# An earlier place for the first attention scores, the query and key norms and the first output unit in a two-block float32 kernel

## The chip, the cores and the metric

One core of a Trainium2 chip runs the whole program in one launch. The metric is the device time of one execution in microseconds; the median over several executions is compared. The five engines named below are TensorE (matrix products into PSUM), VectorE, ScalarE, GpSimd and SyncE (which here only issues DMAs). Each has a queue of its own, worked in the order written; they meet at semaphores.

## The reference

The reference is float32 throughout, on 256 tokens of width 1024. A first block has two layers, a second block one; each is a mixer followed by a gated feed-forward layer (SwiGLU, hidden width 2816), with RMS norms and residuals. The change lies in the first layer's mixer, `hybrid_mixer`:

```python
proj = h @ w_in
gq, gk, gv, gr, glr, sq, sk, sv = jnp.split(proj, cuts, axis=-1)
o_gla = gla_mixer(gq, gk, gv, gr, glr, w_gate2, b_gate, g_gla)
o_sb = stick_breaking_mixer(sq, sk, sv, g_q, g_k)
o = jnp.concatenate([o_gla, o_sb], axis=-1)
return o @ w_out
```

`gla_mixer` is a gated linear attention with 4 heads, chunks of 64, an RMS norm over each head's output and a gate `silu(r)`. `stick_breaking_mixer` has 8 heads of 64 and is computed like this, for blocks of 128 queries:

```python
qh = _rms_f32(heads(q), g_q) * (SB_HEAD_DIM ** -0.5)
kh = _rms_f32(heads(k), g_k)
z = jnp.einsum('bhtd,bhsd->bhts', qh[:, :, q0:kv_len], kh[:, :, :kv_len])
log_keep = jnp.where(past, jax.nn.log_sigmoid(-z), 0.0)
between = lax.cumsum(log_keep, axis=3, reverse=True) - log_keep
w = jnp.where(past, jnp.exp(jax.nn.log_sigmoid(z) + between), 0.0)
outs.append(jnp.einsum('bhts,bhsd->bhtd', w, vh[:, :, :kv_len]))
```

## The kernel before, in words

**Weights.** All weights come as a stream of units of 128 x 2048 float32 (1 MB). SyncE loads unit u into one of two raw slots once VectorE has made the low half of unit u - 2 (`lo_done`, L1089). ScalarE then copies it to a rounded high half (`hi`, L260), which for units from 3 on waits until TensorE has finished unit u - 2 (`unit_done`, L259), since there are three slots. VectorE subtracts to give the low half (`lo`, L264). Each product is done three times, high by high, high by low and low by high (L277 to L279), to keep float32 precision. A unit of projections or output has two halves of 24 products each.

**The stages around the change.** Units 0 to 11 are the projections (`in1`), 12 to 15 the output matrix of the mixer (`out1(0)` to `out1(3)`), and from 16 on the feed-forward layer. The stick-breaking heads are worked in four pairs g. Projections 8 and 9 hold the keys of the pairs and 10 and 11 the queries, two pairs to a unit. These four units are numbered j = 0 to 3 in `qk_ss`, `qk_rstd` and `qk_norm` ("the sums j = 3", "factor 3"; the norm of unit 11 is j = 3). The scores of pairs 0 and 1 need j = 0 and 2, those of pairs 2 and 3 need j = 1 and 3.

- `qk_ss(j)` (L1154): TensorE sums the squares of 64 rows, one product of 512 columns. `qk_rstd(j)` (L1701): ScalarE takes Ln and Exp (L1704, L1707), "factor j". `qk_norm(j)` (L2108): VectorE scales projection 8 + j into `QKN` (L2112). Before that VectorE copies the projection out of PSUM (`copy_proj`, L2105), and the squares are made by ScalarE (`qk_square`, L1698) or, for j = 3, by VectorE (L2167).
- The GLA output `OG` is squared by ScalarE (L1747), summed by TensorE (L1215, "the GLA sums"), goes through Ln and Exp (L1752, L1754) on ScalarE, and is scaled and gated on VectorE (L2162, L2174); `gla_high(j)` (L2206) makes the high half of a quarter of the mixer's output.
- `sb_z(g)` (L1221): scores of pair g into PSUM banks `SB_BANK[g]` and the next. `sb_log(g)` (L1759): Abs, Exp and Ln on ScalarE (L1765, L1768, L1770), "logs g". `sb_keep(g)` (L2181): VectorE, two operations (L2187, L2190), "keep". `sb_between(g)` (L1239): TensorE adds the sums over later keys (L1242, L1244), "the correction" (the first is g = 0, the third g = 2). `sb_logs(g)` (L2192): VectorE (L2196), "log g". `sb_weights(g)` (L1772): Exp on ScalarE (L1774). `sb_out(g)` (L1248): weights times values on TensorE; `sb_store(g)` (L1778): ScalarE copies it into `MIX`.
- `mix_split_lo(dve, 0, (q,))` (L660): the low half of MIX quarter q. `out1(j, ks)` (L1260): the products of output unit j for the input tiles ks, two tiles to a quarter, 12 products to a quarter; it waits for that quarter's low half and for the unit's low half (L1263).
- `idle_products(7, 10)` (L1278): ten bfloat16 products on zeros into a bank that nobody reads.

**What sets the order.** Nothing is scheduled by a program: each engine's order is written out by hand, TensorE's at L1210 to L1299, ScalarE's at L1740 to L1800, VectorE's at L2157 to L2225. After it, the residual of each output unit is added by VectorE (L2247), which with ScalarE also makes the operands of the feed-forward layer (L452, L569). GpSimd issues its first loads (L2602 to L2605) when the last quarter of the mixer's output is there (`act_lo` at 8, L2600).

Of the kernel before, what the change touches and what calls it, by code (L numbers as in the profile page):

```python
# [74 lines left out]
def program(nc, A):  # L75
# [6 lines left out]
    with ExitStack() as ctx:  # L82
        sems = {}

        def S(name):
            if name not in sems:
                sems[name] = ctx.enter_context(nc.semaphore(name))
            return sems[name]
# [47 lines left out]
        def banks(a, b):  # L136
            return PS[:, a:b, :].rearrange("p b n -> p (b n)")
# [129 lines left out]
        def hi(act, u):  # L267
            if u < UNITS:
                split_hi(act, u, u % SLOTS, u % RAW_SLOTS, u // RAW_SLOTS + 1)
# [11 lines left out]
        def idle_products(bank, n):  # L281

            for _ in range(n):
                nc.tensor.matmul(PS[:, bank, :], zero[:, 0:P], zero, start=True, stop=True)
# [60 lines left out]
        FOLDED = {0: "mixn0", 1: "ffnn0", 2: "mixn1", 3: "ffnn1"}  # L345
        HALF = {0: 0, 1: 0, 2: 0, 3: 0}
        MIX_HALF = (1, 0)
        OUT1_BANK = (7, 2, 3, 0)
        SB_BANK = (0, 2, 4, 0)
        NORM_HN = {4: 0, 5: 1, 6: 2}  # L350
        NORM_ROW = {4: 0}
        BACK_BANK = ((5, 7, 0, 2), (4, 5, 7, 6))
# [746 lines left out]
        def _(pe):  # L1099
# [42 lines left out]
            def in1(u, middle=None):  # L1142

                pe.wait_ge(S("lo_done"), u + 1)
                if u >= 4:
                    pe.wait_ge(S(f"proj{u % 2}_copied"), u // 2)
                outs = [PS[:, IN1_BANK(u), t * T:(t + 1) * T] for t in range(2)]
                if u in (6, 7):
                    last = token_unit(u % SLOTS, [(0, t, outs[t]) for t in range(2)], None, middle)
                else:  # L1150
                    last = feature_unit(u % SLOTS, outs, 0, middle=middle)
                last.then_inc(S("unit_done"), 1)

            def qk_ss(j):  # L1154

                pe.wait_ge(S("qk_sq"), j + 1)
                if j == 0:
                    pe.wait_ge(S("norm_rs"), 1)
                if j == 1:
                    pe.wait_ge(S("qk_rs"), 1)  # L1160
                if j >= 2:
                    pe.wait_ge(S(f"proj{j % 2}_copied"), 6)
                nc.tensor.matmul(PS[:, QK_BANK[j], :], blk, SQF[:, j * 512:(j + 1) * 512], start=True, stop=True)\
                    .then_inc(S("qk_ss"), 1)
# [43 lines left out]
                                         start=True, stop=True)  # L1208
            i.then_inc(S("gla_mm"), 1)
            qk_ss(0)  # L1210
            in1(10)

            pe.wait_ge(S("gla_act"), 5)
            for e in range(2):
                i = nc.tensor.matmul(PS[:, e, :], ones, OR[:, e * 512:(e + 1) * 512], start=True, stop=True)  # L1215
            i.then_inc(S("gla_mm"), 1)
            qk_ss(1)
            in1(11, middle=lambda: qk_ss(2))


            def sb_z(g):  # L1221
                if g == 0:
                    pe.wait_ge(S("qkn_done"), 3)
                    pe.wait_ge(S("og_rs"), 1)
                if g == 1:
                    pe.wait_ge(S("gla_act"), 4)
                if g == 2:
                    pe.wait_ge(S("qkn_done"), 4)
                if g == 3:
                    pe.wait_ge(S("sb_lz2"), 1)  # L1230
                for e in range(2):
                    r, b = half(e), SB_BANK[g] + e
                    kT, qT = QKN[r, g * T:(g + 1) * T], QKN[r, 1024 + g * T:1024 + (g + 1) * T]
                    nc.tensor.matmul(PS[:, b, 0:256], kT[:, 0:P], qT, start=True, stop=False, skip_group_check=True)
                    i = nc.tensor.matmul(PS[:, b, 256:384], kT[:, P:T], qT[:, P:T], start=False, stop=False,
                                         skip_group_check=True)
                i.then_inc(S("sb_z"), 1)

            def sb_between(g):  # L1239
                pe.wait_ge(S("sb_keep"), g + 1)  # L1240
                for e in range(2):
                    nc.tensor.matmul(PS[:, SB_BANK[g] + e, 0:384], minus, SBM[:, g % 2, e, :], start=False, stop=False,  # L1242
                                     skip_group_check=True)
                    i = nc.tensor.matmul(PS[:, SB_BANK[g] + e, 128:256], minus_all, SBM[:, g % 2, e, 256:384],  # L1244
                                         start=False, stop=True, skip_group_check=True)
                i.then_inc(S("sb_between"), 1)
# [13 lines left out]
            def out1(j, ks, blocks=range(2)):  # L1260

                u, b = U_OUT1 + j, OUT1_BANK[j]
                pe.wait_ge(S("lo_done"), u + 1)  # L1263
                if 0 in ks and j:
                    pe.wait_ge(S("sb_lz2"), 4 if j == 3 else 2)
                for nb in blocks:
                    for k in ks:
                        wait_act(pe, "o1", k)
                        H, L = wblk(u % SLOTS, nb * KT + k)
                        i = split_mm(PS[:, b, nb * T:(nb + 1) * T], H, L, a_hi[:, k, 1, :], a_lo[:, k, 1, :],  # L1270
                                     k + nb == 0, k == KT - 1, skip_group_check=True)
                if KT - 1 in ks:
                    i.then_inc(S("unit_done"), 1)

            sb_z(0)
            sb_z(1)
            qk_ss(3)
            idle_products(7, 10)  # L1278
            sb_between(0)
            sb_z(2)  # L1280
            sb_z(3)
            sb_out(0)
# [8 lines left out]
            out1(0, (4, 5))  # L1291
            out1(1, (4, 5))
            sb_out(3)
            out1(2, range(4))
            out1(2, (4, 5))
            for j in range(3):
                out1(j, (6, 7))
            out1(3, range(KT))
            ffn_pe(pe, 0, "ffn0", 1)  # L1299

# [345 lines left out]
        def _(act):  # L1646
# [49 lines left out]
            def qk_square(j):  # L1696
                act.wait_ge(S(f"proj{j % 2}_copied"), (8 + j) // 2 + 1)
                nc.scalar.activation(SQF[:, j * 512:(j + 1) * 512], PROJ[:, 8 + j, :], ACT.Square)\  # L1698
                    .then_inc(S("qk_sq"), 1)

            def qk_rstd(j):  # L1701
                r = RSF[:, j * 512:(j + 1) * 512]
                act.wait_ge(S("qk_ss"), j + 1)
                nc.scalar.activation(r, PS[:, QK_BANK[j], :], ACT.Ln, scale=1.0 / 64, bias=prm_eps)\  # L1704
                    .then_inc(S("qk_rs"), 1)
                act.wait_ge(S("qk_rs"), 2 * j + 1)
                nc.scalar.activation(r, r, ACT.Exp, scale=-0.5).then_inc(S("qk_rs"), 1)  # L1707
# [38 lines left out]
            act.wait_ge(S("gla_act"), 4)  # L1746
            nc.scalar.activation(OR, OG, ACT.Square).then_inc(S("gla_act"), 1)  # L1747
            qk_rstd(0)
            qk_square(2)
            hi(act, 13)  # L1750
            act.wait_ge(S("gla_mm"), GLA_MM["sums"])
            nc.scalar.activation(OR, banks(0, 2), ACT.Ln, scale=1.0 / P, bias=prm_eps).then_inc(S("og_rs"), 1)  # L1752
            act.wait_ge(S("og_rs"), 1)
            nc.scalar.activation(OR, OR, ACT.Exp, scale=-0.5).then_inc(S("og_rs"), 1)  # L1754
            qk_rstd(1)
            qk_rstd(2)


            def sb_log(g):  # L1759

                l = SBL[:, g % 2]
                act.wait_ge(S("sb_z"), g + 1)
                if g >= 2:
                    act.wait_ge(S("sb_v"), g - 1)
                nc.scalar.activation(l, PS[:, SB_BANK[g]:SB_BANK[g] + 2, 0:384], ACT.Abs)\  # L1765
                    .then_inc(S("sb_a"), 1)
                act.wait_ge(S("sb_a"), 3 * g + 1)
                nc.scalar.activation(l, l, ACT.Exp, scale=-1.0).then_inc(S("sb_a"), 1)  # L1768
                act.wait_ge(S("sb_a"), 3 * g + 2)
                nc.scalar.activation(l, l, ACT.Ln, bias=1.0).then_inc(S("sb_a"), 1)  # L1770
# [11 lines left out]
                act.wait_ge(S("sb_o_read"), 2 * (j - 1))  # L1782

            sb_log(0)
            qk_rstd(3)
            sb_log(1)
            sb_weights(0)
            sb_log(2)
            sb_weights(1)
            sb_store(0)  # L1790
# [274 lines left out]
        def _(dve):  # L2065
# [91 lines left out]
            lo(dve, 12)  # L2157
            copy_proj(10)
            qk_norm(0)
            lo(dve, 13)  # L2160
            dve.wait_ge(S("og_rs"), 2)
            dve.scalar_tensor_tensor(OG, OG, prm("glan"), OR, ALU.mult, ALU.mult).then_inc(S("gla_step"), 1)  # L2162
            qk_norm(1)
            qk_norm(2)
            copy_proj(11)
            dve.wait_ge(S("proj1_copied"), 6)
            dve.tensor_tensor(SQF[:, 3 * 512:4 * 512], PROJ[:, 11, :], PROJ[:, 11, :], ALU.mult).then_inc(S("qk_sq"), 1)  # L2167
            dve.wait_ge(S("gla_step"), 3)
            dve.wait_ge(S("gla_act"), 2)
            og = OG.rearrange("p (e a t) -> p a e t", e=2, a=2)  # L2170
# [32 lines left out]
            def gla_high(j):  # L2203
                ks = slice(2 * j, 2 * j + 2)
                dve.wait_ge(S("gla_out"), 1)
                dve.tensor_copy(mix_operands(0, ks)[0], MIX[:, ks, :]).then_inc(S("mix_hi"), 1)  # L2206

            sb_keep(0)
            qk_norm(3)
            gla_high(0)  # L2210
            dve.wait_ge(S("sb_bias"), 2)
            sb_logs(0)
            sb_keep(1)
            gla_high(1)
            mix_split_lo(dve, 0, (0,))
            sb_logs(1)
            mix_split_lo(dve, 0, (1,))
            sb_keep(2)
            sb_logs(2)
            sb_keep(3)  # L2220
# [546 lines left out]
```

## Time and profile before

| | us |
|---|---|
| median of 3 runs | 1015.05 |
| lowest, highest | 1014.77, 1016.3 |
| the profiled execution | 1014.54 |
| its span, first to last instruction | 1012.4 |
| TensorE busy | 995.6 (98%) |
| VectorE busy | 664.4 (66%) |
| ScalarE busy | 489.6 (48%) |
| chain that ended last | TensorE 93%, VectorE 3%, ScalarE 2%, DMA 1% |

Times in the trace count from the start of the span. The rows name an engine (PE is TensorE, PEld its weight loads, DVE VectorE, ACT ScalarE, POOL GpSimd, SPq the DMA queue of SyncE), the line of the kernel, what is written and read, and what ended a wait. Matrix products overlap: a product of 256 columns has a duration of 0.28 us, and the next one starts 0.12 us after it. The granted clock of TensorE is given as a share of full speed, 2.4 GHz.

### The profile page before, as it was taken

Reading aid. Unit: us, or ns where it says so; the run is one execution under the profiler, and the core shown is the slowest. Engines: PE = TensorE matmul, PEld = TensorE weight load, DVE = VectorE, ACT = ScalarE, POOL = GpSimd, SP = SyncE. Lnnn points to the kernel's source line nnn. Section 1 sums busy time; section 2 is a strip of 40 time slices with the busy share of each in tenths; the row PEclk is TensorE's granted clock in tenths of the full one; section 3 lists DMA queues with packets and bytes.
Section 4 is the critical chain, followed back from the end, with each engine's and each line's share of the span. In section 5 each row is a group of like instructions: output and inputs, shape, how many; then the busy total and the mean of one; then the engine's idle time right before and its main releaser. Section 6 shows DMA issues by size and latency. Waiting matters only on the chain.

```text
span 1012.4 us, 14616 instructions
## 1 busy us (share of the span) xinstructions
PE 995.6 (98%) x6164; PEld 845.7 (84%) x6168; DVE 664.4 (66%) x751; ACT 489.6 (48%) x578; POOL 29.7 (3%) x59
## 2 busy tenths in 40 slices
PE   9999999999999999999999999999999999999997
PEld 7997888888888987988888887989978988888886
DVE  5566487767677766767777776434765666666664
ACT  6467474443436533845443547333456454344443
POOL 0000000000000000001010110000000000000000
PEclk9999999999999999999999999999999999999999
DMA  7642367767665654347888883722101435655451
GB/s 268 225 160 91 110 225 271 244 218 254 222 241 187 208 182 129 125 173 272 282 288 276 308 292 119 280 99 91 43 1 43 146 119 184 216 188 206 167 208 42
DMA packets 33751, 187.33 MB, mean 185 GB/s; under 512 B 3744, under 2 KB 7584, under 8 KB 15136
## 3 DMA queue, kind: packets, MB, share of 16 engines
q1 hardware_dynamic: 25344, 154.82, 44.1%
q0 software_dynamic: 7344, 27.79, 7.8%
q10 hardware_dynamic: 1008, 3.94, 1.0%
q8 instruction: 41, 0.67, 0.3%
q14 instruction: 14, 0.11, 0.0%
HBM read 181.41 MB, written 1.05 MB: 180 GB/s over the span
## 4 chain that ended last, share of the span: by engine, by line
PE 93%; DVE 3%; ACT 2%; DMA 1%; issue 0%; SPq 0%; DVEq 0%; ACTq 0%
PE PS L711 11%; PE PS L713 11%; PE PS L712 11%; PE PS L277 7%; PE PS L278 7%; PE PS L279 7%; PE PS L766 6%; PE PS L764 6%; PE PS L765 6%; PE PS L1309 2%; PE PS L744 1%; PE PS L329 1%; PE PS L315 1%; PE PS L330 1%; PE PS L331 1%; DMA raw<-wstream 1%
## 5 line engine op out<-in xcount | busy, mean ns | idle before, releaser
L264 DVE TENSOR_TENSOR w_lo<-raw,w_hi 128x2048 fp32r<-128x2048 f32 x140 | 320.6, 2291 | 174.3 <-ACT w_hi L260 151.7
L260 ACT ACTIVATE w_hi<-raw 128x2048 fp32r<-128x2048 f32 x129 | 246.4, 1912 | 144.0 <-DMA raw<-wstream 110.7
L711 PE MATMUL PS<-w_hi,a_hi 128*128 128x512 f32 x512 | 202.5, 396 | 0.0
L713 PE MATMUL PS<-w_hi,a_lo 128*128 128x512 f32 x512 | 199.8, 390 | 0.0
L712 PE MATMUL PS<-w_lo,a_hi 128*128 128x512 f32 x512 | 199.5, 390 | 0.0
L277 PE MATMUL PS<-a_hi,w_hi 128*128 128x256 f32 (+1 forms) x496 | 150.0, 302 | 1.8 <-DVE w_lo L264 1.5
L278 PE MATMUL PS<-a_lo,w_hi 128*128 128x256 f32 (+1 forms) x496 | 147.1, 297 | 0.0
L279 PE MATMUL PS<-a_hi,w_lo 128*128 128x256 f32 (+1 forms) x496 | 147.0, 296 | 0.0
L713 PEld LDWEIGHTS PS<-w_hi,a_lo 128*128 128x128 f32 x512 | 96.1, 188 | 20.5
L712 PEld LDWEIGHTS PS<-w_lo,a_hi 128*128 128x128 f32 x512 | 96.2, 188 | 19.1
L711 PEld LDWEIGHTS PS<-w_hi,a_hi 128*128 128x128 f32 x512 | 96.2, 188 | 18.8
L764 PE MATMUL PS<-w_hi,h_hi 128*128 128x512 f32 x264 | 103.2, 391 | 0.0
L766 PE MATMUL PS<-w_lo,h_hi 128*128 128x512 f32 x264 | 102.8, 389 | 0.0
L765 PE MATMUL PS<-w_hi,h_lo 128*128 128x512 f32 x264 | 102.7, 389 | 0.0
L277 PEld LDWEIGHTS PS<-a_hi,w_hi 128*128 128x128 f32 x496 | 94.7, 191 | 8.0 <-issue 3.5
L278 PEld LDWEIGHTS PS<-a_lo,w_hi 128*128 128x128 f32 x496 | 94.8, 191 | 3.2 <-issue 0.7
L279 PEld LDWEIGHTS PS<-a_hi,w_lo 128*128 128x128 f32 x496 | 94.8, 191 | 2.5
L937 DVE CUSTOM_DVE_ANT_0 MODJ<-modraw,CROW 128x1024 f32<-128x1024 f32 x64 | 77.9, 1217 | 0.6 <-DMA modraw<-wmod 0.3
L766 PEld LDWEIGHTS PS<-w_lo,h_hi 128*128 128x128 f32 x264 | 49.5, 188 | 10.4
L764 PEld LDWEIGHTS PS<-w_hi,h_hi 128*128 128x128 f32 x264 | 49.6, 188 | 10.3 <-issue 0.2
L765 PEld LDWEIGHTS PS<-w_hi,h_lo 128*128 128x128 f32 x264 | 49.6, 188 | 10.1
L866 ACT ACTIVATE h_hi<-PS 128x512 fp32r<-128x512 f32 x33 | 19.7, 596 | 67.5 <-PE PS L744 67.5
(363 smaller groups left out, 1231.4 us busy)
## 6 DMA issues: line engine op xcount, KB each, us to landing
raw<-wstream SPq DMA_DIRECT2D x141, 1024.0 KB, 4.8
modraw<-wmod POOLq DMA_DIRECT2D x48, 512.0 KB, 5.1
U<-CU SPq DMA_DIRECT2D x28, 142.0 KB, 2.8
cst<-cst ACTq DMA_DIRECT2D x1, 1440.0 KB, 10.2
mlw<-mlw ACTq DMA_DIRECT2D x1, 1280.0 KB, 5.9
X<-xT SPq DMA_DIRECT2D x2, 512.0 KB, 4.9
raw<-wstream SPq DMA_DIRECT2D x2, 512.0 KB, 7.7
CROW<-crow POOLq DMA_DIRECT2D x1, 1024.0 KB, 5.2
```

Source lines behind the costliest of these rows:

```text
L260: nc.scalar.activation(w_hi[:, slot, :], raw[:, rslot, :], ACT.Copy).then_inc(S("hi_done"), 1)
L264: dve.tensor_tensor(w_lo[:, slot, :], raw[:, rslot, :], w_hi[:, slot, :].bitcast(F32), ALU.subtract).then_inc(S("lo_done"), 1)
L277: nc.tensor.matmul(out, H, xh, start=start, stop=False, **kw)
L278: nc.tensor.matmul(out, H, xl, start=False, stop=False, **kw)
L279: return nc.tensor.matmul(out, L, xh, start=False, stop=stop, **kw)
L711: nc.tensor.matmul(out, a_hi[:, k, src, ts], wh, start=k == 0, stop=False, skip_group_check=True)
L712: nc.tensor.matmul(out, a_hi[:, k, src, ts], wl, start=False, stop=False, skip_group_check=True)
L713: i = nc.tensor.matmul(out, a_lo[:, k, src, ts], wh, start=False, stop=k == KT - 1, skip_group_check=True)
L764: nc.tensor.matmul(out, hh, wh, start=False, stop=False, skip_group_check=True)
L765: nc.tensor.matmul(out, hl, wh, start=False, stop=False, skip_group_check=True)
L766: return nc.tensor.matmul(out, hh, wl, start=False, stop=False, skip_group_check=True)
L937: dve.tensor_tensor_reduce(out=MODJ, in0=modraw[:, n % 2, :], in1=CROW[:, c, :], scale=1.0, scalar=0.0, op0=ALU.mult, op1=ALU.add, accum_o ...
```

## The change

On TensorE, the sums j = 1 move from behind unit 10 into its middle, the sums j = 2 from the middle of unit 11 to before it, the scores of pairs 0 and 1 from behind unit 11 into its middle, and the first correction goes ahead of the sums j = 3. The products on zeros are taken out. The last quarter of output unit 0 is done in the middle of output unit 2. The waits of `sb_z` are handed over to match the swapped PSUM banks. On ScalarE, factors 1 and 2 go ahead of the second half of the GLA norm, and the high half of unit 13 and factor 3 go behind logs 1. On VectorE, norms 1 and 2 go ahead of the GLA norm, `gla_high(0)` ahead of the first keep, the copy and squares of unit 11 behind that keep, norm 3 behind the second keep, and the low half of unit 13 behind the low half of MIX quarter 1.

```diff
-        OUT1_BANK = (7, 2, 3, 0)
-        SB_BANK = (0, 2, 4, 0)
+        OUT1_BANK = (7, 0, 1, 2)
+        SB_BANK = (2, 0, 4, 2)
...
             qk_ss(0)
-            in1(10)
+            in1(10, middle=lambda: qk_ss(1))
 
             pe.wait_ge(S("gla_act"), 5)
             for e in range(2):
                 i = nc.tensor.matmul(PS[:, e, :], ones, OR[:, e * 512:(e + 1) * 512], start=True, stop=True)
             i.then_inc(S("gla_mm"), 1)
-            qk_ss(1)
-            in1(11, middle=lambda: qk_ss(2))
-
+            qk_ss(2)
 
             def sb_z(g):
                 if g == 0:
                     pe.wait_ge(S("qkn_done"), 3)
+                    pe.wait_ge(S("gla_act"), 4)
+                if g == 1:
                     pe.wait_ge(S("og_rs"), 1)
-                if g == 1:
-                    pe.wait_ge(S("gla_act"), 4)
                 if g == 2:
                     pe.wait_ge(S("qkn_done"), 4)
...
-            sb_z(0)
-            sb_z(1)
+            def first_two():
+                sb_z(0)
+                sb_z(1)
+
+            in1(11, middle=first_two)
+            sb_between(0)
             qk_ss(3)
-            idle_products(7, 10)
-            sb_between(0)
             sb_z(2)
             sb_z(3)
             sb_out(0)
...
             sb_out(3)
-            out1(2, range(4))
-            out1(2, (4, 5))
-            for j in range(3):
-                out1(j, (6, 7))
+            out1(2, range(3))
+            out1(0, (6, 7))
+            out1(2, range(3, 6))
+            out1(1, (6, 7))
+            out1(2, (6, 7))
             out1(3, range(KT))
             ffn_pe(pe, 0, "ffn0", 1)
...
             nc.scalar.activation(OR, OG, ACT.Square).then_inc(S("gla_act"), 1)
             qk_rstd(0)
+            qk_rstd(1)
             qk_square(2)
-            hi(act, 13)
             act.wait_ge(S("gla_mm"), GLA_MM["sums"])
             nc.scalar.activation(OR, banks(0, 2), ACT.Ln, scale=1.0 / P, bias=prm_eps).then_inc(S("og_rs"), 1)
+            qk_rstd(2)
             act.wait_ge(S("og_rs"), 1)
             nc.scalar.activation(OR, OR, ACT.Exp, scale=-0.5).then_inc(S("og_rs"), 1)
-            qk_rstd(1)
-            qk_rstd(2)
...
             sb_log(0)
+            sb_log(1)
+            hi(act, 13)
+            sb_weights(0)
             qk_rstd(3)
-            sb_log(1)
-            sb_weights(0)
             sb_log(2)
...
             qk_norm(0)
-            lo(dve, 13)
+            qk_norm(1)
+            qk_norm(2)
             dve.wait_ge(S("og_rs"), 2)
             dve.scalar_tensor_tensor(OG, OG, prm("glan"), OR, ALU.mult, ALU.mult).then_inc(S("gla_step"), 1)
-            qk_norm(1)
-            qk_norm(2)
-            copy_proj(11)
-            dve.wait_ge(S("proj1_copied"), 6)
-            dve.tensor_tensor(SQF[:, 3 * 512:4 * 512], PROJ[:, 11, :], PROJ[:, 11, :], ALU.mult).then_inc(S("qk_sq"), 1)
...
+            gla_high(0)
             sb_keep(0)
-            qk_norm(3)
-            gla_high(0)
+            copy_proj(11)
+            dve.wait_ge(S("proj1_copied"), 6)
+            dve.tensor_tensor(SQF[:, 3 * 512:4 * 512], PROJ[:, 11, :], PROJ[:, 11, :], ALU.mult).then_inc(S("qk_sq"), 1)
             dve.wait_ge(S("sb_bias"), 2)
             sb_logs(0)
             sb_keep(1)
+            qk_norm(3)
             gla_high(1)
             mix_split_lo(dve, 0, (0,))
             sb_logs(1)
             mix_split_lo(dve, 0, (1,))
+            lo(dve, 13)
             sb_keep(2)
```

## Rows read from the trace of the kernel before

**Rows 1.** List of waits, TensorE: in total, times, longest (us).
```profile
PE PS L310 <- ACT a_hi L531: 1.6, 1, 1.6
```

**Rows 2.** Timeline of TensorE: start, duration (us), [idle before, releaser].
```profile
93.36 2.10 PE L284 MATMUL PS<-zero 128*128 128x512 bf16 x9
95.89 0.91 PE L1242 MATMUL PS<-SBM,csb 128*128 128x384 f32 x2 [0.43 <-DVE SBM L2190]
...
99.02 0.71 PE L1234 MATMUL PS<-QKN 64*128 64x256 f32 x4 [0.27 <-DVE SBZ L2196]
...
104.44 0.36 PE L277 MATMUL PS<-a_hi,w_hi 128*128 128x256 f32 x1 [0.32 <-DVE a_lo L660]
...
105.95 0.91 PE L1242 MATMUL PS<-SBM,csb 128*128 128x384 f32 x2
...
128.56 0.39 PE L277 MATMUL PS<-a_hi,w_hi 128*128 128x256 f32 x1 [1.52 <-DVE w_lo L264]
...
134.41 0.40 PE L711 MATMUL PS<-w_hi,a_hi 128*128 128x512 f32 x1
```

**Rows 3.** The chain that ended last, in order of time: start, us.
```profile
81.47 1.72 PE PS L1215 x4
83.19 0.86 PE PS L1163 x2
...
97.67 0.23 PE PS L1244 x2
...
102.48 0.23 PE PS L1244 x2
```

**Rows 4.** Timeline of ScalarE, columns as in rows 2.
```profile
84.57 1.10 ACT L1752 ACTIVATE OR<-PS,epsc 128x1024 f32<-128x1024 f32 x1
...
86.67 0.67 ACT L1704 ACTIVATE RSF<-PS,epsc 128x512 f32<-128x512 f32 x1
87.37 0.64 ACT L1707 ACTIVATE RSF<-RSF 128x512 f32<-128x512 f32 x1
...
91.56 0.81 ACT L1765 ACTIVATE SBL<-PS 128x768 f32<-128x768 f32 x1 [2.31 <-PE PS L1235]
...
99.00 0.84 ACT L1774 ACTIVATE SBZ<-SBZ 128x768 f32<-128x768 f32 x1 [1.19 <-DVE SBZ L2196]
...
133.49 1.92 ACT L260 ACTIVATE w_hi<-raw 128x2048 fp32r<-128x2048 f32 x1 [2.87 <-DMA raw<-wstream]
```

**Rows 5.** Timeline of VectorE, columns as in rows 2.
```profile
84.70 2.29 DVE L264 TENSOR_TENSOR w_lo<-raw,w_hi 128x2048 fp32r<-128x2048 f32 x1 [1.84 <-ACT w_hi L260]
...
92.01 1.28 DVE L2174 TENSOR_TENSOR MIX<-OG,RSG 128x512 f32<-128x512 f32 x2
...
94.15 0.96 DVE L2187 SCALAR_TENSOR_TENSOR SBM<-PS,SBL 128x768 f32<-128x768 f32 x1 [0.57 <-ACT SBL L1770]
95.14 0.69 DVE L2190 TENSOR_TENSOR SBM<-SBM,csb 128x512 f32<-128x512 f32 x1
95.75 0.74 DVE L2112 SCALAR_TENSOR_TENSOR QKN<-PROJ,epsc,RSF 128x512 f32<-128x512 f32 x1
...
98.00 0.96 DVE L2196 SCALAR_TENSOR_TENSOR SBZ<-PS,SBBIAS 128x768 f32<-128x768 f32 x1 [1.17 <-PE PS L1244]
...
103.62 0.68 DVE L660 TENSOR_TENSOR a_lo<-MIX,a_hi 128x512 fp32r<-128x512 f32 x1
```

**Rows 6.** DMA issues: size, median us from issue to landing.
```profile
CTX<-ctxT POOLq DMA_DIRECT2D x1, 1024.0 KB, 8.6
```

**Rows 7.** Timeline of TensorE at the start and the end of the span.
```profile
1.21 4.45 PE L284 MATMUL PS<-zero 128*128 128x512 bf16 x10 [1.21 <-DVE epsc L2067]
...
1006.61 0.39 PE L766 MATMUL PS<-w_lo,h_hi 128*128 128x512 f32 x1
```

**Rows 8.** Windows at the end: engines' busy time, granted clock, DMA share, GB/s.
```profile
1010.00:1010.25 0.25, 0.00 (x0) 0.00 (x0) 0.00 (x0) 0.00 (x0) 0.00 (x0) 1.00 1.01 385
...
1010.50:1011.00 0.50, 0.00 (x0) 0.00 (x0) 0.00 (x0) 0.00 (x0) 0.00 (x0) 0.50 1.02 385
```

## The prediction

> **What bounds the kernel now.** The page says that TensorE is busy for 98% of the span, so time can only be won where it waits or runs work that nobody needs. The list of waits comes next: its longest entry for TensorE is 1.6 us [rows 1]. Then TensorE's timeline through the stretch of the change [rows 2], where the waits get their places. It shows 2.10 us of products on zeros from 93.36 (nine of the ten have a record), and the first correction product at 95.89 after a wait of 0.43; then waits of 0.27 at 99.02, 0.32 at 104.44, and 1.52 at 128.56, the last for the low half of weight unit 15. Zero products and waits together are 4.6 us: more than that the change can't win. Last, the chain of waits [rows 3] and the timelines of ScalarE [rows 4] and VectorE [rows 5], for the duration of each step that feeds TensorE. The profiled execution took 1014.54 us around a span of 1012.4; the median of the runs is 1015.05, 0.5 above it. I work out a difference in span and add it to the median.
>
> **What goes.** The zero products go, with the 0.43 behind them: 2.53 us. The 1.52 at 128.56 goes too. Unit 15's high half waits until output unit 0 is finished, then 1.92 us (ScalarE [rows 4]) and 2.29 (VectorE [rows 5]) pass, 4.3 with the hand-overs, before output unit 3 can start. The 48 products of output unit 3 take 128.56 to 134.41, 0.12 each. Before, 24 of them lay over these 4.3 us (2.9); now 42 do, 5.1: covered, with 0.8 us to spare. The new order of the output products costs nothing else.
>
> **Part one: norms forward.** The sums of squares j = 1 move into the middle of unit 10; TensorE's work is the same, unit 10 ends 0.86 later (one such product, 83.19 [rows 3]), at 82.33, and the GLA sums (1.72) at 84.05. The sums j = 2 now follow at once. Their input needs VectorE's copy of unit 10 and ScalarE's square, two operations on 512 columns, like those of 0.6 to 0.75 us in rows 4 and 5: some 1.4 of the 1.72, so it is ready. They end at 84.91, the first half of unit 11 (24 products) at 87.78. Meanwhile ScalarE takes the Ln of the GLA sums (1.10), Ln and Exp of factor 2 (86.67 to 88.00 before, 1.33 [rows 4]) and VectorE the norm (0.74 [rows 5]): from 84.07, ready at 87.2. The first scores don't wait; they end at 88.7 and the second pair's by 89.5, so unit 11 ends at 92.3.
>
> **Part two: the first correction.** From Abs on ScalarE (91.56) to the start of VectorE's keep (94.15) took 2.59 us [rows 4, 5], now 88.68 to 91.27; keep took 94.15 to 95.83, now to 92.95. The GLA gating and its copy, ahead of it on VectorE from 87.4, are two steps like that of 1.28 and short ones, and fit. TensorE, free at 92.3, waits 0.7 and runs the correction from 93.0 to 95.0 (95.89 to 97.90 before [rows 2, 3]). Here the kernel is 2.9 us ahead.
>
> **Part three: what is late next.** TensorE's next two items are the sums j = 3 (0.86, to 95.85) and the scores of pair 2, which need the norm of unit 11. Before, that norm was through at 96.5 [rows 5], while TensorE was in the first correction. Now it stands behind the correction on both engines. ScalarE's queue reads: logs 1 (to 93.7), high half of unit 13 (to 95.5), weights 0, factor 3. Weights 0 wait for VectorE's log 0 (0.96, 95.0 to 95.95) and take 0.84, to 96.8; factor 3 takes 1.33, to 98.1; the norm 0.74, to 98.85. So TensorE stands from 95.85 to 98.9: **3.05 us**. Pair 2's scores start 1.0 later than before (97.90, behind the correction). The whole lead is gone. The 0.27 at 99.02 goes as well: log 0 is done long before.
>
> **Part four: the low half of unit 13.** From pair 3's scores to the end of the second correction took 99.02 to 102.71, 3.69 us [rows 2, 3]; with 0.85 for pair 2's scores (97.90 to 98.75, where the 0.27 at 99.02 begins [rows 2, 3]) ahead of it, that is 98.9 to 103.4. VectorE then has log 1 (0.96), the low part of MIX quarter 1 (0.68), the moved low half of unit 13 (**2.29**, which lay at 84.70, where VectorE would have waited), and only then pair 2's keep (1.68): hand-overs and overlaps included, to 108.7. TensorE has 24 output products in between and the small wait for quarter 1, 3.24 us before (102.71 to 105.95), and is free at 106.65. It waits **2.1 us**, until 108.75; before, the row at 105.95 has no wait. All output products stand behind that one.
>
> **The DMAs and queues.** Unit 15's load waits on SyncE's queue for the low half of unit 13, so it is issued at 107.1 instead of 87.0; a load takes some 5 us (issued at 128.5 and awaited until 133.49 for unit 17 [rows 4]) and this one is wanted at 124.9: hidden, with 13 us to spare. GpSimd's first four loads go with the last output quarter, some 2.8 us later, and are wanted only in the FFN. ScalarE's moved high half of unit 13 lies in time in which ScalarE would wait for log 0: nothing.
>
> **The sum.** The third correction moves from 105.95 to 108.75, +2.8; behind it lies work without a wait up to output unit 3, whose wait of 1.52 goes: +1.3. Counted by waits: new 0.70 + 3.05 + 2.1 = 5.85, gone 2.53 + 0.27 + 1.52 = 4.32, +1.5. The two differ by rounded hand-overs; I take the first, which has fewer terms. Output unit 3 then ends at 135.7 in place of 134.41, and all that follows moves with it: **+1.3 us, 1016.4 us**. The forecast's own range is +0.5 to +2.1 (hand-overs of 0.1 in eight steps), 1015.5 to 1017.2.
>
> **The clock.** The wait of 3.05 is twice the longest of before, and the products that kept TensorE at work are gone. No pause of that length lies within the work. After the last product, which ended at 1007.0, the granted clock stayed at 1.00 until 1010.25 and then fell to 0.50, 1.2 GHz [rows 7, 8]: a pause of 3.25, just longer than this one. What the low clock takes: the ten zero products at the start ran at 0.445 us each, against 0.233 at 93.36 [rows 7, 2], and lasted 4.4 us, so 2.2 of them were lost. Lower bound nothing, upper bound one such stretch for each long wait, 4.4. I take nothing, since 3.05 us lies on the side of rows 7 and 8 that kept the clock. The Trainium skill (TensorE: Matmul & The Clock Gate, "Why this matters for your kernels") speaks against this change: pauses between bursts of products must stay short, or the array goes back to its cold clock. By that rule the change would end near +3.5 instead of +1.3.
>
> **Rivals.** (a) The clock falls in the wait of 3.05. For: nothing fills it any more, and a wait of 0.7 lies shortly before. Against: the row of the end. Time: 1.3 + 2.2, 1018.6; chance 0.22. (b) The FFN's start slips. Unit 17's load is issued at 129.1, when unit 15's low half is done, now in the midst of GpSimd's loads, one of which took 8.6 us to land [rows 6]. At 8.6 it lands at 137.7; high half, low half, the last residual and its operands take 1.9 + 2.3 + 0.7 + 1.8: 144.4. TensorE wants them 30 products of 512 columns after 135.7, at 142.6: 1.8 more, 1018.2. Against: the 5 us landing of before, amid the same traffic. Chance 0.10. (c) Faster: the queues don't bind. If factor 3 and the low half of unit 13 find gaps that I don't see, the new waits fall to 0.7 and the time to 1015.05 + 0.7 - 4.6, 1011.2. It counts as faster once the new waits sum to less than 2.6 us (4.6 less 2.0). Against: both long waits follow from the written order and from rows. Chance 0.07. (d) The new order of products does not relieve unit 15, because a hand-over eats the 0.8 us of cover: up to 1.5 is not won, 1016.4 to 1017.9; chance 0.06. The forecast keeps 0.55.
>
> **Numbers.** A measurement of this kernel tells about 0.2%, 2.0 us, from no change. Faster: (c), 0.07. Slower: (a), (b) and 0.04 from the tail of the forecast and of (d), 0.36. Same: 0.57. The range 1015.0 to 1019.0 takes in the forecast, (a), (b) and (d), and leaves out (c).
>
> **What would show it.** Right: no zero products near 93; waits of TensorE near 3 us ahead of pair 2's scores, for VectorE's norm, and near 2.1 ahead of the third correction, for the keep; none ahead of output unit 3; the FFN's first product near 135.7. Wrong in part four: pair 2's keep done before 106.6. A granted clock under 1.00 between 96 and 110 is (a); a wait in the FFN's second unit is (b). Long waits that sum to under 4.3 us would make the forecast's sign wrong.

## The result and the profile after

| | before | changed |
|---|---|---|
| median of 6 runs, us | 1014.92 | 1020.56 |
| lowest | 1014.64 | 1017.86 |
| ratio, 95% interval | | 1.0046 (1.0036 to 1.0057) |
| profiled execution, its span | 1014.54, 1012.4 | 1020.29, 1018.1 |

The change makes the kernel slower by 0.46%, 4.7 us by the ratio (of mean times), 5.7 us between the two spans. That is outside my range, which ended at 1019.0. Two slow executions, one of the changed kernel (1421.36, mean granted clock 0.653) and a later one of the kernel with both cures (1666.48, 0.556), are in the medians and in no ratio; without the first the changed kernel's median is 1020.29. Between the two profiled executions nearly all of the difference arises in the first 160 us; the table shows how far the changed kernel is behind at five places of TensorE.

| TensorE reaches | before | changed | behind |
|---|---|---|---|
| first sums of squares (j = 0) | 74.6 | 74.4 | -0.2 |
| third correction | 105.95 | 110.30 | 4.35 |
| first product of the FFN | 134.4 | 137.0 | 2.6 |
| first transposes of the FFN | 153.1 | 158.8 | 5.7 |
| last product | 1006.6 | 1012.4 | 5.8 |

First the list of waits of the changed kernel, for TensorE (in total, times, longest, in us):

```profile
PE PS L1232 <- DVE QKN L2113: 3.2, 1, 3.2
PE PS L1240 <- DVE SBM L2187: 2.6, 2, 2.0
PE PS L711 <- DVE a_lo L569: 2.2, 1, 2.2
PE PS L310 <- ACT a_hi L531: 1.6, 1, 1.6
```

Three entries stand above the one that led the list before [rows 1]: the scores of pair 2, the third correction, and the FFN's second unit. TensorE's timeline puts them in place (start, duration, wait before); it answers to [rows 2]:

```profile
92.84 0.91 PE L1240 MATMUL PS<-SBM,csb 128*128 128x384 f32 x2 [0.59 <-DVE SBM L2187]
...
98.85 0.71 PE L1232 MATMUL PS<-QKN 64*128 64x256 f32 x4 [3.15 <-DVE QKN L2113]
...
106.59 0.36 PE L277 MATMUL PS<-a_hi,w_hi 128*128 128x256 f32 x1 [0.32 <-DVE a_lo L660]
...
110.30 0.91 PE L1240 MATMUL PS<-SBM,csb 128*128 128x384 f32 x2 [2.05 <-DVE SBM L2187]
...
137.00 0.40 PE L711 MATMUL PS<-w_hi,a_hi 128*128 128x512 f32 x1
...
144.87 0.47 PE L711 MATMUL PS<-w_hi,a_hi 128*128 128x512 f32 x1 [2.25 <-DVE a_lo L569]
```

The zero products and the wait ahead of output unit 3 are gone. The scores of pair 2 start at 98.85, the very time worked out, after 3.15 us. The third correction waits 2.05, but starts 1.5 later than worked out. What lies between is in the windows (width, busy time of TensorE, its weight loads, VectorE, ScalarE, GpSimd, then the granted clock, DMA share and GB/s):

```profile
96.00:98.00 2.00, 0.00 (x0) 0.00 (x0) 1.46 (x2) 1.97 (x3) 0.00 (x0) 1.00 0.00 0
98.00:100.00 2.00, 1.15 (x11) 1.12 (x13) 1.69 (x3) 0.18 (x2) 0.00 (x0) 0.95 0.03 8
100.00:102.00 2.00, 2.00 (x14) 1.40 (x12) 0.00 (x0) 1.94 (x3) 0.00 (x0) 0.50 0.00 0
102.00:104.00 2.00, 2.00 (x11) 1.30 (x8) 0.00 (x0) 0.40 (x1) 0.00 (x0) 0.70 0.00 0
```

The granted clock fell to 0.50, 1.2 GHz, close to 99.9, **when TensorE had been at work again for a microsecond**, and came back within the last window. ScalarE's timeline shows the third wait's origin, as the row at 133.49 did before [rows 4]:

```profile
139.10 1.92 ACT L260 ACTIVATE w_hi<-raw 128x2048 fp32r<-128x2048 f32 x1 [5.81 <-DMA raw<-wstream]
```

Unit 17 was awaited until 139.10. Its load had been issued behind the low half of unit 15, at 130.7: 8.4 us to landing, in place of 5. The low half of unit 15 on VectorE and the first of GpSimd's loads, before and then changed:

```profile
126.21 2.29 DVE L264 TENSOR_TENSOR w_lo<-raw,w_hi 128x2048 fp32r<-128x2048 f32 x1 [1.25 <-ACT w_hi L260]
120.42 0.66 POOL L2602 DMA_DIRECT2D CROW<-crow  x1 [119.96 <-DVE a_lo L660]
...
128.41 2.29 DVE L264 TENSOR_TENSOR w_lo<-raw,w_hi 128x2048 fp32r<-128x2048 f32 x1 [1.25 <-ACT w_hi L260]
124.78 0.67 POOL L2603 DMA_DIRECT2D CROW<-crow  x1 [124.32 <-DVE a_lo L660]
```

From GpSimd's first load to the issue of unit 17's it was 8.1 us before (120.4 to 128.5) and 5.9 in the changed kernel (124.8 to 130.7).

### The profile page after: what moved, and what is told of

The parts are those of the page before. It is cut to its first block, busy times and chain, and to the rows that moved or that the text cites. A ratio compares the mean times of both kernels' runs of the same rounds, so it can differ in the third digit from the quotient of the medians.

```text
span 1018.1 us, 14597 instructions
## 1 busy us (share of the span) xinstructions
PE 994.3 (98%) x6155; PEld 845.3 (83%) x6158; DVE 664.2 (65%) x751; ACT 490.3 (48%) x578; POOL 29.7 (3%) x59
## 4 chain that ended last, share of the span: by engine, by line
PE 87%; DVE 5%; ACT 4%; DMA 3%; issue 1%; SPq 0%; DVEq 0%; ACTq 0%
PE PS L711 11%; PE PS L713 11%; PE PS L712 11%; PE PS L277 6%; PE PS L279 6%; PE PS L278 6%; PE PS L764 6%; PE PS L766 6%; PE PS L765 6%; DMA raw<-wstream 3%; PE PS L1310 2%; DVE w_lo L264 2%; ACT w_hi L260 1%; PE PS L744 1%; PE PS L315 1%; PE PS L310 1%
```

## The experiments

They form three groups of four, each on one chip, beside the kernel before, whose median was 1016.38, 1015.09 and 1015.24 in the three groups. So I read ratios and profiles, and times only within a group. Theory A from here on: three separate losses, the waits of the written order (+1.3), the clock, and the landing of unit 17.

### Fill the long wait

```diff
             qk_ss(3)
+            idle_products(7, 12)
             sb_z(2)
```

> The changed kernel with twelve products on zeros (2.7 us) in the wait ahead of pair 2's scores. Theory A (the loss has three parts: new waits of the written order +1.3, the clock that falls in the 3.15 us wait +1.5, the late landing of unit 17 +2.3 and more): the granted clock stays at 1.00 up to the end of the third correction, output unit 3 ends 1.3 to 1.6 us earlier than in the changed kernel, the wait in the FFN's second unit stays near 2.2, and the time is 1018.0 to 1019.0. Rival B (all of the loss beyond +1.3 comes of the clock, the FFN's wait with it): the FFN's wait goes too and the time is near 1016.3. Rival C (the fall costs nothing, since other waits take it up): no change, 1020.5.

Ratio 1.0045 (1.0028 to 1.0062), 1020.07 against 1016.38. That misses A's 1018.0 to 1019.0 and by the time alone looks like rival C; but on this chip the kernel before took 1.5 more than in the first measurement. Its timeline of TensorE:

```profile
100.82 0.71 PE L1232 MATMUL PS<-QKN 64*128 64x256 f32 x4 [0.57 <-DVE QKN L2114]
...
110.68 0.91 PE L1240 MATMUL PS<-SBM,csb 128*128 128x384 f32 x2 [2.04 <-DVE SBM L2188]
...
144.95 0.47 PE L711 MATMUL PS<-w_hi,a_hi 128*128 128x512 f32 x1 [1.95 <-DVE a_lo L569]
```

The clock stayed at 1.00. From pair 2's scores to the third correction it took 9.86 us here and 11.45 in the changed kernel (98.85 to 110.30), so this fall cost 1.6 us, which speaks against rival C. The FFN's wait stays at 1.95, which refutes rival B. The intervals of the two kernels overlap, so the gain of filling is shown by the profile and not by the times: this execution had reached its first sums of squares 2.0 us late (76.4), which is nothing of the edit.

### Hold GpSimd's loads back

```diff
             pool.wait_ge(S("act_lo"), 8)
+            pool.wait_ge(S("raw_loaded1"), 144)
```

> The changed kernel with GpSimd's first four loads held back until unit 17 has landed. Theory A (unit 17's load shares the DMA engines with them): unit 17 lands in about 4.8 us instead of 8.4, the wait of 2.25 in the FFN's second unit goes, the fall of the clock stays, and the time is 1017.5 to 1018.5. Rival B (the FFN's wait comes of the clock's fall): the wait stays, 1020.5. Rival D (the loads are wanted early in the FFN, so that holding them back opens a new wait there): the landing is short but the time stays at 1019.5 or more.

Ratio 1.0026 (1.0013 to 1.0038), 1018.58, just above A's range and below rival D's. TensorE has no wait at all between 120 and 160: the wait of 2.25 is gone, and rival B falls a second time. The profiled execution shows the other loss at a worse place than before; the clock's windows:

```profile
98.00:101.00 3.00, 1.52 (x10) 1.36 (x11) 1.81 (x4) 0.63 (x1) 0.00 (x0) 0.60 0.02 5
101.00:104.00 3.00, 3.00 (x19) 2.08 (x17) 0.00 (x0) 2.50 (x3) 0.00 (x0) 0.50 0.00 0
```

Here the clock stayed low from within the wait of 3.16 on, and the way from the scores (99.48) to the third correction (112.14) took 12.66 us, 2.8 more than with the filled wait. It fell once more behind the second wait. So what the falling clock cost at the scores was 1.6 us in one execution and 2.8 in another, where it stayed low for about twice as long.

### The new order of output products alone, in the kernel before

```diff
-            out1(2, range(4))
-            out1(2, (4, 5))
-            for j in range(3):
-                out1(j, (6, 7))
+            out1(2, range(3))
+            out1(0, (6, 7))
+            out1(2, range(3, 6))
+            out1(1, (6, 7))
+            out1(2, (6, 7))
```

> The kernel before with the new order of the output products alone. Theory A: the wait of 1.52 ahead of output unit 3 goes, but unit 17's load is now issued 2.3 us earlier, into GpSimd's loads, and lands in 6 to 8 us, so that the FFN's second unit waits about 1 to 1.5: time 1014.3 to 1015.0. Rival E (this part is a clean gain): no wait in the FFN's second unit, 1013.4.

Ratio 1.0010 (1.0002 to 1.0019): not a gain but a small loss, barely clear of none. The list of waits of TensorE from 120 to 160 us:

```profile
PE PS L711 <- DVE a_lo L569: 2.1, 1, 2.1
PE PS L604 <- DVE SQ L580: 0.4, 1, 0.4
```

The wait of 1.52 has gone and 2.1 + 0.4 has come in its place. Rival E is refuted; I had set A's own wait too small, at 1 to 1.5, and its time too low.

### The zero products alone, taken out of the kernel before

```diff
             qk_ss(3)
-            idle_products(7, 10)
             sb_between(0)
```

> The kernel before without its ten products on zeros; TensorE then pauses 2.6 to 2.8 us there. Theory A (a pause must be about as long as the changed kernel's 3.15 to lower the clock): the clock stays at 1.00 and the time at 1015.0. Rival F (a pause of 2.7 is enough in some executions): the granted clock is 0.50 for a stretch behind it in some runs, and these take 1 to 2 us more, 1016 to 1017.

Ratio 1.0011 (1.0001 to 1.0020), 1017.14 against 1016.38.

```profile
96.23 0.91 PE L1242 MATMUL PS<-SBM,csb 128*128 128x384 f32 x2 [2.58 <-DVE SBM L2189]
```

The profiled execution paused 2.58 us and kept its clock. Of the 11 executions, 8 had a mean granted clock of 0.997 or 0.998, against 2 of the 29 of the kernel before on that chip. A mean of 0.998 can come from the idle end of the program alone (see "Unit 13's low half ahead of log 1"); one of 0.997 can't by any end seen here, and 3 of the 11 had it, against none of the 76 executions of the kernel before in the three groups. So the clock falls more often without the zero products, which goes against theory A, though no trace shows such a fall at this pause. By the ratio, again barely clear of none, the zero products paid for themselves, by about 0.1%. For the condition of rival F, that such an execution takes 1 to 2 us more, the times on this chip spread too far.

### Both cures together

The first two edits in one kernel.

> The changed kernel with the products on zeros of the first experiment and GpSimd's loads held back as in the second. Theory A: only the waits of the written order are left, 0.6 ahead of the first correction, zero products and a rest of 0.5 ahead of pair 2's scores, 2.05 ahead of the third correction, none in the FFN's second unit: 1.0 to 1.6 us over the kernel before. Rival G (something else makes the changed kernel slower as well): 2.5 or more over it.

Ratio 1.0021 (1.0010 to 1.0031), 1018.24 against 1015.09. This is more than A's 1.6 and looks like rival G. The trace says otherwise. TensorE's timeline at the third correction:

```profile
109.33 1.44 PE L1240 MATMUL PS<-SBM,csb 128*128 128x384 f32 x2 [2.04 <-DVE SBM L2188]
```

And the windows from there on, columns as above:

```profile
108.00:110.00 2.00, 0.67 (x2) 0.38 (x3) 1.24 (x2) 0.49 (x1) 0.00 (x0) 0.90 0.61 147
110.00:112.00 2.00, 2.00 (x6) 1.36 (x5) 0.00 (x0) 0.00 (x0) 0.00 (x0) 0.50 0.89 377
```

The clock fell at the **other** wait, of 2.04 us. Ten of its executions divide in the same way. Three had a mean clock of 0.999 or 1.000 and took 1015.74 to 1016.47, 0.7 to 1.4 over the kernel before: the forecast of +1.3, undisturbed. Seven had 0.996 to 0.998 and took 1017.08 to 1019.76; for the five of them at 0.998 the mean alone doesn't prove a fall within the work. A was right about the waits and wrong in thinking that one filled wait cures the clock.

### Unit 13's low half ahead of log 1

In the same kernel:

```diff
             mix_split_lo(dve, 0, (0,))
+            lo(dve, 13)
             sb_logs(1)
             mix_split_lo(dve, 0, (1,))
-            lo(dve, 13)
             sb_keep(2)
```

> The same, and VectorE's low half of unit 13 placed ahead of log 1, where VectorE waits 3.6 us for the second correction. Theory A: the wait of 2.05 ahead of the third correction goes, all else stays, so 0.4 to 1.0 us under the kernel before and 2.0 under the kernel without this step. Rival H (ScalarE's logs 2 end late and hold the keep anyway): the wait stays above 1.

Ratio 0.9987 (0.9976 to 0.9997), 1014.31: 0.8 under the kernel before, and 3.9 under the kernel without this step where 2.0 were expected. TensorE's wait ahead of the third correction is gone, and rival H with it. 8 of 11 executions had a mean granted clock of 0.999 or 1.000, against 3 of 10; of the other three, one is listed at 0.948, which its time of 1017.43 doesn't bear out. VectorE's 2.29 us cost 2.05 of waiting and nearly as much again, for which falls of the clock are the likely cause, not shown one by one.

How the mean has to be read is shown by the profiled execution, which is listed at 0.998. Its clock never fell within the work, only behind the last product:

```profile
1007.59 0.39 PE L766 MATMUL PS<-w_lo,h_hi 128*128 128x512 f32 x1
...
1010.00:1010.25 0.25, 0.00 (x0) 0.00 (x0) 0.05 (x1) 0.01 (x1) 0.00 (x0) 0.99 0.24 66
1010.25:1010.50 0.25, 0.00 (x0) 0.00 (x0) 0.00 (x0) 0.00 (x0) 0.00 (x0) 0.50 0.00 0
```

The fall came 2.3 us after the last product here and stood until the end of the span at 1014.3, which costs nothing and lowers the mean by 0.002.

### The scores of pairs 2 and 3 behind the second correction

```diff
             qk_ss(3)
-            sb_z(2)
-            sb_z(3)
             sb_out(0)
             sb_between(1)
+            sb_z(2)
+            sb_z(3)
...
             mix_split_lo(dve, 0, (1,))
-            lo(dve, 13)
             sb_keep(2)
+            lo(dve, 13)
```

and GpSimd's loads held back; no zero products.

> The changed kernel with pair 0's output and the second correction ahead of the scores of pairs 2 and 3, the low half of unit 13 behind pair 2's keep, and GpSimd's loads held back; no products on zeros. Theory A: TensorE has work while norm 3 is made, its longest pause there is 1.2 us, the clock stays at 1.00, the third correction starts near 103.5 in the changed kernel's count (110.3 there), and the time is 2 to 4 us under the kernel before. Rival I (the later scores of pairs 2 and 3 hold the third and fourth corrections): a wait of 2 or more stands ahead of one of these, and the time is that of the kernel before.

Ratio **0.9968 (0.9955 to 0.9980)**, 1012.51 against 1015.09: the fastest kernel of the study, 2.6 us under the one before. Its timeline of TensorE:

```profile
97.33 0.66 PE L1253 MATMUL PS<-SBZ,PROJ 128*64 128x256 f32 x4 [1.13 <-ACT SBZ L1774]
...
100.07 0.71 PE L1232 MATMUL PS<-QKN 64*128 64x256 f32 x4
...
105.39 0.91 PE L1240 MATMUL PS<-SBM,csb 128*128 128x384 f32 x2 [0.59 <-DVE SBM L2187]
```

Pair 2's scores come 1.2 later than in the changed kernel, and TensorE doesn't stand for them, since it has pair 0's output and the second correction to do while norm 3 is made. The third correction starts at 105.39 where it was 110.30. No pause in this stretch is longer than 1.13, and the mean clock was 0.999 or 1.000 in five of six executions. I had expected the third correction near 103.5; the way from pair 2's scores through logs 2 and the keep is longer than I had counted, and the wait of 0.59 for it is rival I in small.

### Outputs and loads in the kernel before

The third and the second edit in the kernel before.

> The kernel before with the new order of the output products and GpSimd's loads held back until unit 17 has landed. Theory A (the wait of 1.52 only moved into the FFN's second unit because unit 17 landed late): neither wait is there, 1.5 us under the kernel before. Rival E2 (the second unit's operands are late for another reason): a wait of 1 to 2 us stays in the FFN's second unit, and the time is that of the kernel before.

Ratio 0.9974 (0.9964 to 0.9985), 1012.97, 2.1 us under the kernel before. TensorE has no wait from 120 to 160, which refutes rival E2. The same order of outputs that lost 0.10% alone gains 0.26% once GpSimd's loads are out of the way.

This also tells what the earlier norms and scores are worth. The fastest kernel has them on top of these two edits and is only 0.5 faster, with overlapping intervals (0.9955 to 0.9980 against 0.9964 to 0.9985). In the profiles, the FFN's first product comes 59.8 us after the first sums of squares in the kernel before, 58.1 here and 57.2 in the fastest kernel. So the earlier norms and scores are worth about 0.9 us in these profiles, and that only with the scores of pairs 2 and 3 moved back as well.

### GpSimd's loads alone, in the kernel before

> The kernel before with GpSimd's loads held back and nothing else. Theory A (they cost time only where unit 17's load falls into them and its slack is gone, and here it had slack): within 0.5 us of the kernel before, so that all that the kernel with both steps gained, 2.1, needs the new order of the outputs as well. Rival J (holding them back is worth something by itself): 0.6 to 1.0 us under it.

Ratio 1.0001 (0.9988 to 1.0013): theory A held. The two edits are worth nothing or less each, and 2.1 us together.

### The later scores with GpSimd's loads at their old place

> The fastest kernel so far (scores of pairs 2 and 3 behind the second correction) with GpSimd's loads at their old place. Theory A: unit 17 lands in about 8 us, a wait of 2 us or more stands in the FFN's second unit, and most of the 2.6 us gain is given back: 0 to 1 us under the kernel before. Rival K (the earlier stretch takes the two loads apart again): no such wait, 2.6 under it.

Ratio 1.0001 (0.9992 to 1.0010): all of the 2.6 us is given back, and rival K is refuted. TensorE's timeline:

```profile
139.11 0.47 PE L711 MATMUL PS<-w_hi,a_hi 128*128 128x512 f32 x1 [2.10 <-DVE a_lo L569]
...
142.50 0.58 PE L604 MATMUL PS<-cst,SQ 128*128 128x1 f32 x4 [0.41 <-DVE SQ L580]
```

The FFN's waits seem to bring falls of the clock with them: of the 11 executions here 4 had a mean of 0.997, and 4 of 11 with the new order of outputs alone, against none of the 14 of the two kernels with the loads held back (the fastest one, and that with outputs and loads). Neither of the two profiled executions shows such a fall, so its place is not shown.

### The changed kernel again

> The changed kernel once more, beside the others. Theory A: new waits +1.3, one or two falls of the clock at 1.2 to 1.7 us each, FFN wait 2.3: 4.5 to 6 us over the kernel before, and its executions spread over 2 to 5 us with their mean granted clock, the ones at 1.000 or 0.999 being the fastest. Rival L (the first measurement was a bad draw): 3 us or less over it.

Ratio 1.0052 (1.0038 to 1.0065), 1020.77 against 1015.24: 5.5 over it, as theory A had it, and rival L is refuted. The spread is 3.1 us (1019.36 to 1022.45), and the two executions at 0.999 are the fastest. The profile is the valuable part, since this execution kept its clock at 1.00 through the same wait:

```profile
98.76 0.71 PE L1232 MATMUL PS<-QKN 64*128 64x256 f32 x4 [3.16 <-DVE QKN L2113]
...
108.62 0.91 PE L1240 MATMUL PS<-SBM,csb 128*128 128x384 f32 x2 [2.04 <-DVE SBM L2187]
...
143.22 0.47 PE L711 MATMUL PS<-w_hi,a_hi 128*128 128x512 f32 x1 [2.26 <-DVE a_lo L569]
```

The third correction starts at 108.62, forecast 108.75; the FFN's first product at 135.33, forecast 135.7. Counted from the first sums of squares, that is 61.0 us after them against 59.8 before: **+1.2** for the part that I had forecast at +1.3. Up to the first transposes it is +4.2: from the FFN's first product to them it takes 21.8 us in place of 18.7, which is the FFN's waits of 2.26 and 0.40 and 0.4 more behind them.

With this the first profiled execution adds up. From the first sums to the first transposes it was 5.8 us behind (84.35 against 78.53): 1.2 for the written order, 1.6 for the fall of the clock and 3.0 for the late landing of unit 17.

### Unit 13's low half ahead of log 1, alone

> The changed kernel with the low half of unit 13 ahead of log 1, and nothing else. Theory A: the wait of 2.05 ahead of the third correction goes, the waits of 3.15 and in the FFN's second unit stay: 2.0 to 2.6 us faster than the changed kernel, 2.5 to 3.5 over the kernel before. Rival M (what is gained there is lost again in the FFN's second unit, since the load of unit 17 moves deeper into GpSimd's loads): the FFN's wait grows to 3 or more, and less than 1.5 us is gained.

Ratio 1.0038 (1.0026 to 1.0050), 1019.83: only 0.9 faster than the changed kernel beside it, with overlapping intervals, so A's number missed and M's number held. M's mechanism did not: the FFN's wait stayed at 2.22. The windows around that wait show a part of what took the gain in the profiled execution:

```profile
142.00:144.00 2.00, 0.14 (x1) 0.17 (x2) 1.82 (x5) 1.05 (x3) 0.00 (x0) 1.00 0.37 70
144.00:146.00 2.00, 2.00 (x8) 1.65 (x9) 1.97 (x4) 2.00 (x2) 0.00 (x0) 0.84 0.88 360
146.00:148.00 2.00, 2.00 (x7) 1.54 (x6) 1.97 (x3) 0.19 (x1) 0.00 (x0) 0.50 0.23 94
```

The clock fell there too, after it had fallen at the scores. Up to the FFN's first product this execution took 60.4 us from the first sums, against 62.6 in the first profiled execution of the changed kernel, which also had one fall there: these are the 2.2 us that A forecast. From there to the first transposes it lost 0.9 against it, and behind 160 us another 1.4, for which I have no cause. All six executions had a mean clock of 0.995 to 0.997. Why it fell more often here than in the changed kernel beside it (0.996 to 0.999) stays open.

## Why the prediction was wrong, step by step

**What goes, and parts one to four: right.** The zero products and the 1.52 went. Waits of 0.70, 3.05 and 2.1 were forecast and 0.59, 3.15 and 2.05 measured. The sum of +1.3 was +1.2 in the execution of the changed kernel that kept its clock, and +0.7 to +1.4 in those of the kernel with both cures that did. The claim that unit 15 is covered held as well: no wait stands ahead of output unit 3. (The text on the weights says that a high half waits until TensorE has finished unit u - 2. By its own numbering from 0 that is unit u - 3, since L259 waits for a count of u - 2 finished units; the prediction rightly has unit 15 wait for output unit 0, unit 12.)

**The DMAs and queues: failed.** "GpSimd's first four loads go with the last output quarter, some 2.8 us later, and are wanted only in the FFN" asked who waits for these loads, and not whom they disturb. The new order lets unit 15's low half follow closely upon the last output quarter, and with it the load of unit 17 upon GpSimd's. It then lands in 8.4 us instead of 5. Before, the last of GpSimd's loads landed some 2 us after unit 17's was issued (issued at 122.12, 8.6 to landing, against 128.5); in the changed kernel some 5 us after (126.48 and 9.1, against 130.7). Unit 18's load, issued at 134.3, ran beside it too. The five kernels with the new order and the loads at their old place wait 1.95 to 2.26 there; the five with the loads held back don't wait. The Trainium skill (Trainium Kernel Development and Optimization, "Key Constraints") says that transfers from all queues run on the same DMA engines and interleave; the trace agrees, with 8.4 us in place of 5. Rival (b) had this mechanism, but a chance of 0.10, because I took "amid the same traffic" for granted. Its size was too small as well: 1.8, measured 3.0, of which 2.25 + 0.40 are waits. The chain behind the landing was shorter than its 6.7 us (139.10 to 144.87, 5.8), but TensorE wanted the operands 5.6 us after the FFN's first product (137.00 to 142.62), not 6.9.

**The clock: failed.** The step "I take nothing, since 3.05 us lies on the side of rows 7 and 8 that kept the clock" read the pause off the wrong row. Rows 7 and 8 say how long after the last product the fall was recorded at the end of one execution. They don't say what pause is safe. The same idle end had its fall after 2.3 us in the profiled execution with unit 13's low half ahead of log 1 (both cures in it), and after 5.2 in the changed kernel; within the work the fall came a microsecond after the changed kernel had resumed, and in others it followed pauses of 2.04 and 2.22 as well. Its price was forecast at 2.2 and measured at 1.6 and 2.8. The rule of the Trainium skill that I had weighed (TensorE: Matmul & The Clock Gate, "Why this matters for your kernels") spoke for a loss here. The trace agrees in three of the four profiled executions that paused for 3.15 or 3.16 us.

**Rivals as alternatives: failed.** I gave (a) and (b) a sum each, 1018.6 and 1018.2, and ended the range at 1019.0. They arise in different places and came together: 1.3 + 2.2 + 1.8 is 5.3, 1020.35, against a median of 1020.56. That this sum is so near is in part luck, since the clock was priced too high (1.6 in the profiled execution) and the landing too low (3.0).

## What to carry to other kernels

Losses in different places add up, so a range must hold their sum and not the largest of them. A stage that is shortened brings the next stage's load nearer to whatever transfers start at its end: check which loads will now overlap before counting the gain, since here one wait on another queue turned the reordering from a small loss into a gain of 2.1 us. Where TensorE is to wait for a chain through two other engines, give it whatever products are ready, even if their results are wanted later.

## What the runs showed of the hardware

Six falls of the granted clock from 1.00 to 0.50 lie within the work of the profiled executions. One came in the midst of a pause, the other five 0.1 to 1.5 us after TensorE had resumed, so the row of a fall must be read back to the wait before it. The clock fell at the pause of 3.15 or 3.16 us in three profiled executions and was left alone in a fourth. It fell at the pause of 2.04 or 2.05 us in two of five, at the FFN's wait of 1.95 to 2.26 in one of six, and not at one of 2.58. Why it falls in one execution and not in the next stays open. The same kernel thus spreads over several microseconds: with both cures, 1015.74 to 1019.76, the three with a mean granted clock of 0.999 or 1.000 ahead of all others.

The idle end of the program lowers the clock too, between 2.3 and 5.2 us after the last product in these profiles. A mean granted clock of 0.998 over an execution of 1015 us is therefore no proof of a fall that cost time.
